# Latent attention scores: the rope part as 128-row matmuls with a half-zero key

## The reference

```python
def mla_mixer(h, positions, w_in, g_qa, w_qb, g_kva, w_kvb, w_out):
    c_q, c_kv, k_rope, gate = jnp.split(h @ w_in, [512, 1024, 1088], axis=-1)
    q  = (rms_norm(c_q, g_qa) @ w_qb).reshape(B, S, 16, 128 + 64)
    kv = (rms_norm(c_kv, g_kva) @ w_kvb).reshape(B, S, 16, 128 + 128)
    q_nope, q_rope = q[..., :128], q[..., 128:]
    k_nope, v = kv[..., :128], kv[..., 128:]
    q_rope, k_rope = _rope_2(q_rope, cos, sin), _rope_2(k_rope, cos, sin)
    q = concatenate([q_nope, q_rope]);  k = concatenate([k_nope, k_rope for every head])
    s = einsum('bqhd,bkhd->bhqk', q, k) * (128 + 64) ** -0.5    # causal softmax, then times v
```

## Time and profile before

| | us |
|---|---|
| median of 3 runs | 2647.68 |
| lowest and highest | 2646.3, 2649.38 |
| the profiled execution | 2647.79 |
| its span, first to last instruction | 2646.0 |
| TensorE matmul busy in it | 2570.5 |
| VectorE, ScalarE, GpSimd busy | 1666.9, 1310.4, 107.4 |
| TensorE's granted clock, mean | 0.983 of full |

### The profile page before, as it was taken

One profiled execution on the slowest core, in us unless ns is written; L12 is line 12 of the kernel. 1 busy time (PEld: TensorE's weight loads), 2 busy tenths in 40 slices (PEclk: granted clock), 3 DMA queues, 4 the chain that ended last, 5 costly groups with the idle time before them and its releaser, 6 DMA issues.

```text
span 2646.0 us, 40634 instructions
## 1 busy us (share of the span) xinstructions
PE 2570.5 (97%) x14860; PEld 2239.3 (85%) x14860; DVE 1666.9 (63%) x2063; ACT 1310.4 (50%) x1686; POOL 107.4 (4%) x82
## 2 busy tenths in 40 slices
PE   7999999999999999999999999999999997999998
PEld 6888888888888888888888888888888886988886
DVE  6754654566695577777577757785465847655454
ACT  6545444544444555555355535554444554444454
POOL 3000000000000001000000000010001111000000
PEclk9999999999999999999999999999899998999998
DMA  6564666456565656666666666666454553544353
GB/s 205 184 183 136 191 189 188 132 176 175 161 190 144 191 176 189 180 185 187 187 184 183 190 189 185 179 190 180 130 166 128 172 186 108 144 122 128 112 163 107
DMA packets 545507, 442.94 MB, mean 167 GB/s; under 512 B 31241, under 2 KB 542753, under 8 KB 544866
## 3 DMA queue, kind: packets, MB, share of 16 engines
q1 hardware_dynamic: 545186, 441.00, 56.4%
q0 software_dynamic: 192, 0.18, 0.1%
HBM read 439.02 MB, written 2.10 MB: 167 GB/s over the span
## 4 chain that ended last, share of the span: by engine, by line
PE 86%; DVE 7%; ACT 4%; issue 1%; POOL 1%; DMA 1%; SPq 0%; DVEq 0%; ACTq 0%; POOLq 0%
PE blk L648 79%; DVE weight L1678 2%; DVE arena L1678 1%; PE pa L901 1%; ACT weight L1112 1%; ACT arena L1326 1%; PE pa L712 1%; DVE xT L1678 1%; DVE u L1752 1%; DMA weight_raw<-in_w_mem_kv_dram 0%; PE pa L992 0%; DMA weight_raw<-in_w_branch_dram 0%; DVE small L1915 0%; DVE arena L2278 0%; PE pa L703 0%
## 5 line engine op out<-in xcount | busy, mean ns | idle before, releaser
L1678 DVE TENSOR_TENSOR weight<-weight_raw,weight 128x1024 fp32r<-128x1024 f32 (+2 forms) x836 | 1019.5, 1224 | 828.2 <-ACT weight L1112 824.7
L1112 ACT ACTIVATE weight<-weight_raw 128x1024 fp32r<-128x1024 f32 (+2 forms) x836 | 870.4, 1045 | 1033.4 <-PE blk L648 990.6
L648 PE MATMUL blk<-u,weight 128*128 128x512 f32 x5312 | 948.5, 341 | 17.9 <-DVE u L1752 14.5
L648 PEld LDWEIGHTS blk<-u,weight 128*128 128x128 f32 x5312 | 817.2, 190 | 144.0 <-issue 18.0
L648 PE MATMUL blk<-h,weight 128*128 128x512 f32 (+1 forms) x5344 | 929.2, 335 | 4.1 <-DVE h L1678 4.1
L648 PEld LDWEIGHTS blk<-h,weight 128*128 128x128 f32 x5344 | 806.1, 189 | 117.1 <-issue 5.0
L648 PE MATMUL blk<-weight,h 128*128 128x256 f32 (+4 forms) x1952 | 312.1, 321 | 0.0
L648 PEld LDWEIGHTS blk<-weight,h 128*128 128x128 f32 x1952 | 278.4, 190 | 31.7 <-issue 0.3
L648 PE MATMUL blk<-weight,u 128*128 128x512 f32 (+5 forms) x1152 | 210.1, 344 | 4.6 <-DVE weight L1678 4.6
L648 PEld LDWEIGHTS blk<-weight,u 128*128 128x128 f32 x1152 | 181.4, 201 | 29.5 <-DVE weight L1678 5.4
L1678 DVE TENSOR_TENSOR arena<-arena,blk 128x512 f32<-128x512 f32 (+1 forms) x142 | 96.2, 677 | 9.4 <-ACT arena L1164 9.4
(11 more groups left out here) (229 smaller groups left out, 1167.6 us busy)
## 6 DMA issues: line engine op xcount, KB each, us to landing
weight_raw<-in_w_in_dram SPq DMA_DIRECT2D x216, 512.0 KB, 3.6
weight_raw<-in_w_up_dram SPq DMA_DIRECT2D x344, 256.0 KB, 3.2
weight_raw<-in_l_gla_w_in_dram SPq DMA_DIRECT2D x96, 512.0 KB, 3.8
weight_raw<-in_w_down_dram SPq DMA_DIRECT2D x80, 512.0 KB, 3.4
weight_raw<-in_w_branch_dram SPq DMA_DIRECT2D x48, 512.0 KB, 4.0
weight_raw<-in_l_mla_w_in_dram SPq DMA_DIRECT2D x48, 512.0 KB, 3.9
weight_raw<-in_w_mem_kv_dram SPq DMA_DIRECT2D x32, 512.0 KB, 4.3
weight_raw<-in_w_out_dram SPq DMA_DIRECT2D x32, 512.0 KB, 3.4
```

The source lines that it names most:

```text
L648: mm = nc.tensor.matmul(to, lhsT, rhs, start=(kt == 0 and m == 0), stop=(kt == ph.bt - 1 and m == len(ops) - 1))
L1112: nc.scalar.activation(weight_hi[:, r, 0:nk, 0:cols], weight_raw[:, r, 0:nk, 0:cols], ACT.Copy).then_inc(hi_made, 1)
L1678: return nc.vector.tensor_tensor(out_, a, b, op)
```

## The change

The rope matmuls take all 128 rows of the query tile, which hold two heads, and for the key there are two tensors: `k_rope_even` has the key in rows 0 to 63 and zeros in 64 to 127, `k_rope_odd` zeros in rows 0 to 63 and the key in 64 to 127. The other head's query rows meet zeros and add nothing. The count of matmuls, their columns and their order stay. `k_rope_even` has the place of `k_ropeT`; `k_rope_odd` (256 columns) lies over `tri_ge` and `tri_chunk`, which become halves of one tensor `tri`. ScalarE evicts the turned key in two halves in place of one copy. VectorE writes the zeros ahead of the `latent` projection, and TensorE waits for both zeros and both copies before it turns the queries.

```diff
-        tri_ge = sb("tri_ge", [P, P])
-        tri_chunk = sb("tri_chunk", [P, P])
+        tri = sb("tri", [P, 2 * P])
+        tri_ge, tri_chunk = tri[:, 0:P], tri[:, P:2 * P]
...
-        k_rope, k_ropeT = area(4096, NT, 2 * LR), area(17792, S)
+        k_rope_even, k_rope_odd = area(17792, S), tri[:, :]
+        k_rope = area(4096, NT, 2 * LR)
...
             def turn_q():
                 pe.wait_ge(ML["q_roped"], 1)
-                pe.wait_ge(ML["kT"], 1)
+                pe.wait_ge(ML["kT"], 2)
+                pe.wait_ge(ML["zeros"], 2)
                 turn_heads(q_rope, ML["qturned"])
...
                     def ops(h, q, k):
                         c = 4 * g + h
-                        half = slice(0, LR) if h % 2 == 0 else slice(LR, 2 * LR)
-                        return [(q_nope[:, c, q], k_nope[:, c, k]),
-                                (q_ropeT[half, 4 * r + c // 2, q], k_ropeT[half, k])]
+                        own_half = k_rope_even if h % 2 == 0 else k_rope_odd
+                        return [(q_nope[:, c, q], k_nope[:, c, k]), (q_ropeT[:, 4 * r + c // 2, q], own_half[:, k])]
...
-            nc.scalar.activation(k_ropeT, pa[:, 0, 0:S], ACT.Copy).then_inc(ML["kT"], 1)
+            nc.scalar.activation(k_rope_even[0:LR], pa[0:LR, 0, 0:S], ACT.Copy).then_inc(ML["kT"], 1)
+            nc.scalar.activation(k_rope_odd[LR:P], pa[LR:P, 0, 0:S], ACT.Copy).then_inc(ML["kT"], 1)
...
             unit_norm("pre1", range(12, 16), xT, "l1_pre", u_hi, u_lo)
 
+            nc.vector.memset(k_rope_even[LR:P], 0.0).then_inc(ML["zeros"], 1)
+            nc.vector.memset(k_rope_odd[0:LR], 0.0).then_inc(ML["zeros"], 1)
+
             def latent_block(b):
```

More of the change, by code:

```diff
@@ L439, in build_program @@
                                           "hi", "ready", "bias_row")}
-        ML = {x: sem(f"mla_{x}") for x in ("k_roped", "kturned", "kT", "q_roped", "qturned", "qT",
+        ML = {x: sem(f"mla_{x}") for x in ("zeros", "k_roped", "kturned", "kT", "q_roped", "qturned", "qT",
                                           "out", "gated", "hi", "ready")}
@@ L511, in _ @@
             nc.gpsimd.memset(ones[:], 1.0).then_inc(consts, 1)
-            link(nc.gpsimd.memset(tri_ge[:], 1.0))
-            nc.gpsimd.affine_select(out=tri_ge[:], in_=tri_ge[:], compare_op=ALU.is_ge, fill=0.0,
+            link(nc.gpsimd.memset(tri_ge, 1.0))
+            nc.gpsimd.affine_select(out=tri_ge, in_=tri_ge, compare_op=ALU.is_ge, fill=0.0,
                                     base=0, pattern=[[-1, P]], channel_multiplier=1).then_inc(consts, 1)
-            link(nc.gpsimd.memset(tri_chunk[:], 1.0 / GTAU))
-            link(nc.gpsimd.affine_select(out=tri_chunk[:], in_=tri_chunk[:], compare_op=ALU.is_ge,
+            link(nc.gpsimd.memset(tri_chunk, 1.0 / GTAU))
+            link(nc.gpsimd.affine_select(out=tri_chunk, in_=tri_chunk, compare_op=ALU.is_ge,
                                          fill=0.0, base=0, pattern=[[1, P]], channel_multiplier=-1))
@@ L832, in side_sb @@
                     for h in range(4):
-                        nc.tensor.matmul(pa[:, h, 0:S], tri_ge[:], sb_sp[:, h, 0:S], start=True, stop=False)
+                        nc.tensor.matmul(pa[:, h, 0:S], tri_ge, sb_sp[:, h, 0:S], start=True, stop=False)
                         nc.tensor.matmul(pa[:, h, P:S], ones[:], sb_sp[:, h, S:TRI], start=False, stop=True)
-                        mm = nc.tensor.matmul(pa[:, h, S:TRI], tri_ge[:], sb_sp[:, h, S:TRI],
+                        mm = nc.tensor.matmul(pa[:, h, S:TRI], tri_ge, sb_sp[:, h, S:TRI],
                                               start=True, stop=True)
@@ L978, in side_decay @@
                                 pa[:, c // 2, (c % 2) * S + t * P:(c % 2) * S + (t + 1) * P],
-                                g_la[:, t, c * P:(c + 1) * P], tri_chunk[:], start=True, stop=True)
+                                g_la[:, t, c * P:(c + 1) * P], tri_chunk, start=True, stop=True)
                     mm.then_inc(GL["cum"], 1)
```

## The result

The changed kernel took 2630.43 us in the median of 5 runs (2623.97 to 2632.16), the one before 2646.3 in 5 runs (2641.54 to 2649.38); the ratio is 0.9939 (95% interval 0.9921 to 0.9956), so it is faster by 15.9 us or 0.6%. The forecast was 2635.3. The direction and the mechanism were right, the time lies 4.9 us under the forecast and 0.07 us under the lower end of the range.

A forecast was written before the change was run, and what follows sets the result against it. TensorE, busy for 97% of the span, was taken to bound the kernel. From the median of 2647.68 us, 12.4 us saved in four score steps and 0 for the other edits gave 2635.3 us, range 2630.5 to 2641.5.

The forecast's parts named there:

- part 1: In the latent attention's four score steps, 128-row rope matmuls remove row-count changes: 3.1 us a step, 12.4 us in all.
- rows 5: Trace rows of the sparse attention's 128-row score passes: 2.63 us for 16, doubled to 5.25 us for a changed step.
- the exit: The change from a score step back to the projection: removing it exposes one load, counted as 0.10 us won.
- part 2: Behind the score steps ScalarE and VectorE wait for TensorE, so the whole 12.4 us was taken to reach the end.
- rival B: Behind three of four score steps the saving is lost: 2640.0 us if half, 2644.6 us if whole; 7%.
- parts 3 to 5: Two VectorE memsets (0.5 to 1.1 us), a split ScalarE copy (0.38 us more), joined constants: covered or free, 0 us.
- the clock term: TensorE's 7 us low-clock spell at 2526 us, behind the fourth group: taken as unchanged, 3 us either way.
- Rival C: More low clock after waits in the latent attention: two 7 us spells a group lose 24 us, giving 2659 us; 3%.
- Rival A: In score steps loads stay exposed for another reason, such as tensor turns or accumulation: no change, 2647.7 us; 5%.
- The rule against the change: Trainium skill: weight loads overlap matmuls only where row groups differ, so score steps stay about 8.2 us, no change.
- The rule on the tiling mode: Trainium skill: a change of tiling mode drains TensorE; the time is then the forecast's, with 0.20 us for a change.

The follow-up runs named there:

- before: The kernel without the change, its first trace and the runs beside the result: 2646.3 us median of 5 runs.
- before_again: The kernel before, unchanged, run for a second trace and more times: ratio 0.9992 to before.
- rows64_in_after: The changed kernel with all other edits kept, but the rope matmuls at 64 rows again: ratio 0.9996 to before.
- after_padded: The changed kernel plus 14 matmuls of 128 rows by 128 columns ahead of each step's scores, into PSUM columns nothing reads: ratio 0.9999 to before.
- first_phase: The changed kernel with 128-row rope matmuls only in the first two groups, 64 rows in the last two: ratio 0.9976 to before.
- one_phase: The changed kernel with 128-row rope matmuls only in the last two groups, 64 rows in the first two: ratio 0.9968 to before.
- after: The changed kernel, with all edits of the change against before: 2630.43 us, ratio 0.9939.
- after_again: The changed kernel, unchanged, in a further set of runs: ratio 0.9928 to before.
- after_third: The changed kernel, unchanged, in another further set of runs: 2629.5 us, ratio 0.9957 to before.
- nope_first_128: The changed kernel with each group's eight nope matmuls first, then its eight rope matmuls, all 128 rows: 2629.05 us, ratio 0.9952 to before.
- nope_first_64_grouped: The kernel before with its 64-row rope, reordered: nope matmuls first, then rope of heads 0, 2, 1, 3 one behind another: ratio 0.9951 to before.
- nope_first_64_alternate: The kernel before with its 64-row rope, reordered: nope first, then rope of heads 0 and 1 in turn, then 2 and 3: 2628.89 us, ratio 0.994.
- alternate_again: nope_first_64_alternate unchanged, run beside after on the same chip: 2623.98 us, ratio 0.9933 to before.

## Why the prediction was right and wrong

| trace | low clock behind group 4, us | start of first step to start of `mlaout`, us |
|---|---|---|
| before, before_again | 6.8, 3.4 | 188.80, 187.78 |
| rows64_in_after, after_padded | 3.4, 3.4 | 187.92, 187.89 |
| first_phase, one_phase | 6.8, 3.4 | 182.42, 181.70 |
| after, after_again, after_third, nope_first_128 | 3.4, 0, 0, 0 | 175.36, 173.76, 173.72, 173.65 |
| nope_first_64_grouped | 0 | 173.22 |
| nope_first_64_alternate, alternate_again | 3.4, 0 | 171.88, 170.27 |

- **What bounds, and the cost of a change (part 1): right.** Forecast 3.1 us a group and 12.4 in all. At the same low-clock spell of 3.4 us, 187.78 (before_again) less 175.36 (after) is 12.42 us. From one step's start to the next, 35.15 went to 31.95, 80.69 to 77.52. That it fits so closely is in part luck. The step takes 5.05 us where the working from rows 5 had 5.25: it counted 0.22 us for the last pass, but the next line starts 0.03 us behind it (2344.26 and 2344.29, after). So a step is 3.20 us shorter, not 3.00. And the exit, which the forecast counted as 0.10 us won, gives 0.08 back: at the same pace the 96 projection matmuls behind a step take 16.83 us behind 128-row passes and 16.75 behind 64-row ones. That leaves 3.12 us a step. The two slips nearly cancel.
- **Does it reach the end (part 2): right.** The idle times went from 9.6 and 10 us to 6.4 and 6.8, and one_phase shows it for the two groups that rival B doubted. The share of DMA was 0.55 in the third step of after, more than the 0.45 of the earlier trace rows, and TensorE shows no wait for a transfer in that stretch.
- **Memsets, copies, constants (parts 3 to 5): right.** rows64_in_after gives 0.9996. The memsets cost the lower bound, 0.27 us each, and nothing waited for them.
- **The sum: the step that failed is the clock term, which it put at nothing.** The sum took the spell behind the fourth group as unchanged, and the range gave it 3 us either way. In the five traces with a long fourth step it was there each time (6.8, 3.4, 3.4, 3.4 and in first_phase 6.8 us); with a short one it was there in 3 of 8. The average of the four long kernels in the table is 188.1 us, that of the four with 128 rows 174.1: 14.0 us, 12.4 from the step and 1.6 from the spell. Rival C had the sign the other way: fewer, not more. Why the low clock follows the same wait of 3.1 us in front of the values' matmuls less often behind a shorter step stays open; after_padded, dense and long, has the spell, which speaks against the density of the score step as the cause, and thirteen traces are few.
- **The 4.9 us in full.** The forecast starts from 2647.68 us, and the kernel before took 2646.3 in the runs beside the result: 1.4 us. The spell is 1.6 us, by the average of the traces. The other 1.9 us have no cause that the runs show.
- **The range: too narrow, for a spread that it took from three runs.** These differ by 3.1 us. The kernel before taken over the sets has a mean of 2644.6 us in 68 runs, and single runs reach from 2636.3 to 2654.6; a median of five or six runs of after moved from 2625.6 to 2630.4 between sets. The two paces in the projection make up most of what the traces of one kernel differ by. I didn't see them in the one trace of before, where they stand side by side (908 matmuls in 160 us against 867 in 150). On the means, after has 2628.4 us in 16 runs: 16.2 us less. By set it is 16.2, 20.4 and 11.7 us, so the 16.2 are sure to some 2.5 us only (standard error of the three). 14.0 us of it are the stretch. The other 2.2 are not told from zero: outside the stretch the four traces with long steps average 2454.9 us and the four with 128 rows 2452.3, while single ones reach from 2446.0 to 2457.2. after_padded speaks against a cause in the change.
- **Rival A** fell with the result and nope_first_128, **B** with one_phase, **C** with every trace. **The rule against the change** (loads overlap only where row groups differ) is contradicted by every score step of after: all rows, each load 0.11 to 0.21 us ahead. The rule on the tiling mode agrees: two changes in a step leave 0.33 us of idle loads each.

One thing more stands in the traces. The 96 projection matmuls behind a score step also run at one of the two paces, and there the pace goes with what stands in front. Behind 128-row passes they took 16.83 or 16.84 us in all 24 steps, behind the alternating halves 17.05 or 17.06 in all 8, and in the other 64-row orders (before and its like) 16.75 or some 17.07, now the one and now the other. It is worth nothing here, since TensorE's wait for ScalarE in front of the values' matmuls takes it up: behind the first step of after it waits 0.24 us, where before didn't wait. That it is a cause, and how, wasn't tested.

## What to carry to other kernels

Between matmuls that follow each other closely, look at the row counts in the trace: here each change between 64 and 128 rows cost 0.2 us, as much as one pass of 256 columns, and a step of 16 matmuls spent 3.2 of its 8.25 us on it. Keep the count uniform, or, cheaper still, sort: all 128-row matmuls first, then the 64-row ones with the two halves in turn, which ran in pairs here and need no zeros. For a gain under 1%, measure the stretch between two marks in the traces of several executions; the total of this program moves by more than the gain with no edit at all.

## What the runs showed of the hardware

- At a change of row count the next weight load starts with its matmul and not ahead of it, with idle loads of 0.33 us behind a matmul of 256 columns and 0.12 us behind one of 128, and the second fp32 pass comes some 0.1 us later than in a stream of equal rows: 0.2 us in all. A run of 64-row passes on the same rows has no such cost (1.97 us for 16 of 128 columns).
- Passes on rows 0 to 63 and 64 to 127 in turn overlap: 4.22 us against 4.98 for the same work.
- A stream of single-pass projection matmuls has two paces at full clock, 0.173 and 0.176 us a matmul, which one execution takes in one phase and another execution of the same program in the next. What picks the pace is open; behind a score step it went with the rows of the passes in front (24 of 24 and 8 of 8 steps).
- 64 rows of zeros by 256 columns take VectorE 0.27 us, as 32 rows do.
